# One layer of a hybrid diffusion block: another order in the prologue, and another RMSNorm in the tail

## The reference

```python
h = rmsnorm(x) * (1 + scale1) + shift1          # scale, shift, gate: SiLU(c) @ w_mod + b_mod
P = h @ W_in                                    # three token mixers and the merge gates
y_hy  = hyena_mix(...)                          # two long convolutions by FFT, see below
y_gla = gla(...); y_s5 = s5(...)
mix = W_out( sum_b sigmoid(g_b) * (y_b @ W_b) );  x += gate1 * mix
x += gate2 * SwiGLU(rmsnorm(x) * (1 + scale2) + shift2)
out = rmsnorm(x) * g_final

# a long convolution's filter k, for each of the two (cv = 0, 1):
h = (sin(...) @ w3) * exp(-t * |decay|)         # 512 positions x 512 channels, forward and backward
k = k * rsqrt(sum(k * k, axis=positions) + eps) # the filter's norm
k_f = rfft(k)                                   # the filter's spectrum
```

## Time and profile before

| | us |
|---|---|
| median of 3 runs | 1458.78 |
| lowest and highest | 1457.54, 1459.68 |
| profiled execution | 1453.09 |
| its span, first to last instruction | 1450.9 |
| mean granted clock of TensorE | 0.901 of full |

### The profile page before, as it was taken

The page is one execution under the profiler, slowest core; times in us unless marked ns, Lnnn a source line. Parts: engine busy times, 40 slices in busy tenths (PEclk is TensorE's granted clock), DMA queues, the critical chain, the costliest instruction groups (busy, mean ns, idle before and its releaser), DMA issues.

```text
span 1450.9 us, 15211 instructions
## 1 busy us (share of the span) xinstructions
PE 1219.5 (84%) x5929; PEld 919.3 (63%) x5929; DVE 562.8 (39%) x982; ACT 406.3 (28%) x722; POOL 403.3 (28%) x343
## 2 busy tenths in 40 slices
PE   4768998697657888888498989989679999999994
PEld 1335786685445667667364557649468888888883
DVE  3365324645456667566306381323230001100013
ACT  2454212332233333242041110111333222232221
POOL 2003132240211111021031111314135654556541
PEclk9986999798779888998599999989789999999997
DMA  9330132193201112130160214262513323333211
GB/s 331 112 133 0 59 117 75 32 200 121 72 28 50 34 36 80 25 95 20 41 202 15 102 44 145 87 210 80 152 51 88 115 80 93 103 89 115 81 51 58
DMA packets 137714, 131.48 MB, mean 91 GB/s; under 512 B 12985, under 2 KB 125817, under 8 KB 136620
## 3 DMA queue, kind: packets, MB, share of 16 engines
q1 hardware_dynamic: 125280, 103.48, 24.4%
q0 software_dynamic: 4416, 17.50, 3.5%
q10 hardware_dynamic: 7948, 9.54, 2.2%
HBM read 119.49 MB, written 8.91 MB: 89 GB/s over the span
## 4 chain that ended last, share of the span: by engine, by line
PE 56%; DVE 13%; ACT 5%; issue 3%; DMA 0%; ACTq 0%; DVEq 0%; POOL 0%; SPq 0%
PE psum L667 47%; PE psum L886 3%; PE psum L916 1%; PE psum L906 1%; PE psum L919 1%; PE psum L917 1%; PE psum L696 1%; DVE buf L1920 1%; DVE buf L1918 1%; PE psum L718 1%; DVE buf L1919 1%; ACT ring_hi L1339 1%; DVE hT_lo L2172 1%; DVE buf L1897 0%; DVE buf L1898 0%
## 5 line engine op out<-in xcount | busy, mean ns | idle before, releaser
L1185 POOL TENSOR_TENSOR ring_lo<-buf,ring_hi 128x512 fp32r<-128x512 f32 (+2 forms) x260 | 340.3, 1341 | 781.0 <-ACT ring_hi L1339 781.0
L667 PE MATMUL psum<-hT_hi,ring_hi 128*128 128x512 f32 x712 | 294.7, 414 | 25.8 <-POOL ring_lo L1185 15.2
L667 PE MATMUL psum<-hT_lo,ring_hi 128*128 128x512 f32 x712 | 284.1, 399 | 0.0
L667 PE MATMUL psum<-hT_hi,ring_lo 128*128 128x512 f32 x712 | 283.1, 398 | 0.0
L667 PE MATMUL psum<-buf,buf 128*128 128x512 f32 (+1 forms) x480 | 208.5, 589 | 30.3 <-DVE buf L2062 8.9
L1339 ACT ACTIVATE ring_hi<-buf 128x512 fp32r<-128x512 f32 (+2 forms) x260 | 139.7, 611 | 265.9 <-PE psum L667 197.4
L667 PEld LDWEIGHTS psum<-hT_hi,ring_hi 128*128 128x128 f32 x712 | 139.0, 195 | 60.3 <-POOL ring_lo L1185 15.6
L667 PEld LDWEIGHTS psum<-buf,buf 128*128 128x128 f32 x480 | 95.5, 201 | 128.0 <-issue 99.2
L667 PEld LDWEIGHTS psum<-hT_lo,ring_hi 128*128 128x128 f32 x712 | 138.4, 194 | 31.7 <-issue 3.6
L667 PEld LDWEIGHTS psum<-hT_hi,ring_lo 128*128 128x128 f32 x712 | 137.8, 194 | 29.8
L2181 DVE TENSOR_TENSOR buf<-psum,buf 128x512 f32<-128x512 f32 x22 | 15.2, 692 | 224.1 <-PE psum L667 224.1
(11 more groups left out here) (321 smaller groups left out, 1776.6 us busy)
## 6 DMA issues: line engine op xcount, KB each, us to landing
buf<-in_w_in SPq DMA_DIRECT2D x26, 1024.0 KB, 5.3
buf<-in_w_mod SPq DMA_DIRECT2D x24, 1024.0 KB, 6.0
buf<-in_w_ffn_in SPq DMA_DIRECT2D x44, 512.0 KB, 5.1
buf<-in_w_ffn_out SPq DMA_DIRECT2D x8, 1024.0 KB, 5.1
scr_k<-buf POOLq DMA_DIRECT2D x4, 1024.0 KB, 5.8
buf<-scr_k POOLq DMA_DIRECT2D x4, 1024.0 KB, 7.7
buf<-in_w_out SPq DMA_DIRECT2D x4, 1024.0 KB, 7.5
buf<-in_w_ffn_out SPq DMA_DIRECT2D x4, 768.0 KB, 4.4
```

Of the source, the lines that this page charges most:

```text
L667: ins = nc.tensor.matmul(o, a, b, start=start and n == 0, stop=stop and n == len(pairs) - 1)
L1185: nc.gpsimd.tensor_tensor(ring_lo[:, a:a + n], ring[:, a:a + n], ring_hi[:, h + i * n:h + i * n + n].bitcast(fp32), SUB)\
```

## The change

The step list is put in another order at two places, and three computations are written in another way.

**Prologue.** `x_sq` is cut into six calls that ACT issues between the exponentials of the first filter. `rms` stands after block 4 of the modulation, and its scaling of the tokens is a step `xn` of its own after `fnorm` of the first filter. All `modT` steps and `hT` now stand ahead of the first filter's `fspec`. The wait for the token splits moves from `hT` to `chan`. The second `filter` stands behind the k projection, its `fnorm` behind `vhalf(0)`, and its `fspec` behind `vhalf(1)`. `fnorm` now adds the eight squared tiles on DVE (two adds of 128x1024 into `Gp`, then one of 128x1024 and one of 128x512) and makes one product with the matrix of ones.

**Around the second norm.** Blocks 20 to 23 of the modulation and their `gt` steps are interleaved with the four `wo` steps, in the weight ring too, and `A2` follows `wo(0)`. The sum of squares is taken by ACT for each 256 columns as DVE finishes them. `norm2` runs for each token tile inside `wo(3)`. It no longer scales tokens: DVE writes the factor of each token on the diagonal of a 128x128 tile `diag`, and PE multiplies the residual by it, so that one float32 product both transposes and scales. The first four output blocks go token tile by token tile. The first `ffn` job waits for the splits one by one.

**Last products and final norm.** In the last chunk of each `down` the token tile is the outer loop. ACT squares halves of 512 columns after each `down_ev` of the second half, `final` runs for each tile inside the last `down_ev`, its last product is made in two halves, and SP stores each half (256 KB) instead of POOL.

```diff
-                      4: [("x_sq",), ("fnorm", 0)], 5: [("fspec", 0, 0)], 6: [("rms",), ("fspec", 0, 1)]}
+                      4: [("rms",)], 5: [("fnorm", 0), ("xn",)]}
...
-            if i == 4:
-                for k in range(4):
-                    step("modT", k)
...
-        for k in range(4, 8):
+        for k in range(8):
             step("modT", k)
         step("hT")
+        step("fspec", 0, 0)
+        step("fspec", 0, 1)
+        cols_slot("k", K0)
+        step("chan", "k", ("k0", "k1"), True)
         step("filter", 1, 0)
         step("filter", 1, 1)
-        cols_slot("k", K0)
-        step("chan", "k", ("k0", "k1"), True)
-        step("fnorm", 1)
         cols_slot("v0", V0)
         step("vhalf", 0)
+        step("fnorm", 1)
+        cols_slot("v1", V0 + 256)
+        step("vhalf", 1)
         step("fspec", 1, 0)
         step("fspec", 1, 1)
-        cols_slot("v1", V0 + 256)
-        step("vhalf", 1)
...
         for i in range(4):
             want(f"wo{i}", block(I["w_out"][0], 256 * i))
+            want(f"mod{20 + i}", block(w_mod, 256 * (20 + i)), split=False)
             step("wo", i)
-        step("norm2")
-        for i in (20, 21, 22, 23):
-            want(f"mod{i}", block(w_mod, 256 * i), split=False)
-            step("mod", i)
-            step("gt", i)
-        step("A2")
+            step("mod", 20 + i)
+            step("gt", 20 + i)
+            if i == 0:
+                step("A2")
         step("h2T")
...
             def fnorm(cv):
                 pe.wait_ge(S("ones"), 1)
-                pe.wait_ge(S("hsq"), 8 * cv + 8)
+                pe.wait_ge(S("hsum"), cv + 1)
...
-                close(product(o, ((ones, q[:, t, :]) for q in (Gp, Hp) for t in range(4))), name)
+                close(nc.tensor.matmul(o, ones, Gp[:, 0, :], start=True, stop=True), name)
...
             def h2_T():
-                pe.wait_ge(S("xn2"), 4)
-                for k in range(KD):
+                first = [open_job(f"x2T{k}") for k in range(4)]
+                for t in range(4):
+                    pe.wait_ge(S("diag"), t + 1)
+                    for k in range(4):
+                        ins = nc.tensor.matmul(first[k][:, t * P:(t + 1) * P], xr[:, t, k * P:(k + 1) * P],
+                                               diag[:, t, :], start=True, stop=True)
...
+            def x_sq(t):
+                if t == 0:
+                    act.wait_ge(S("x_in"), 32)
+                link(A(sqd, rowsx[t], ACT.Square, accum_out=ssq[:, t:t + 1]))
...
             def fnorm(cv):
+                for t in (0, 2):
+                    dve.wait_ge(S("hsq"), 8 * cv + 2 * t + 4)
+                    go(V.tensor_tensor(Gp[:, t:t + 2, :], Gp[:, t:t + 2, :], Hp[:, t:t + 2, :], ADD))
+                need(cnt[0])
+                link(V.tensor_tensor(Gp[:, 0:2, :], Gp[:, 0:2, :], Gp[:, 2:4, :], ADD))
+                V.tensor_tensor(Gp[:, 0, :], Gp[:, 0, :], Gp[:, 1, :], ADD).then_inc(S("hsum"), 1)
                 evacuated(dve, f"hn{cv}")
...
+            def norm2(t):
+                dve.wait_ge(S("ss2"), 12 + t + 1)
+                V.reduce_sum(ss2[:, t:t + 1], sq2[:, t, :], AX).then_inc(S("ms2"), 1)
+                dve.wait_ge(S("sd2"), t + 1)
+                link(V.reciprocal(rs2[:, t:t + 1], rs2[:, t:t + 1]))
+                V.tensor_scalar(diag[:, t, :], ident, rs2[:, t:t + 1], None, MUL).then_inc(S("diag"), 1)
...
+            def final(t):
+                dve.wait_ge(S("ssf"), 4 + t + 1)
+                V.reduce_sum(ssf[:, t:t + 1], sqf[:, t, :], AX).then_inc(S("msf"), 1)
+                dve.wait_ge(S("sdf"), t + 1)
+                link(V.reciprocal(rsf[:, t:t + 1], rsf[:, t:t + 1]))
+                for h in range(2):
+                    c = slice(512 * h, 512 * h + 512)
+                    V.scalar_tensor_tensor(xr[:, t, c], xr[:, t, c], rsf[:, t:t + 1], gfin[:, c], MUL, MUL)\
+                        .then_inc(S("out"), 1)
```

More of the change, by code:

```diff
@@ L1067, in ffn @@
                     o = open_job(name)
-                    close(product3(o, ((wh[:, k, :], wl[:, k, :], hT_hi[:, k, :], hT_lo[:, k, :])
-                                       for k in range(KD))), name)
+                    for k in range(KD):
+                        if name == "fa0":
+                            pe.wait_ge(S("h_split"), 2 * KD + k + 1)
+                        ins = product3(o, [(wh[:, k, :], wl[:, k, :], hT_hi[:, k, :], hT_lo[:, k, :])],
+                                       start=k == 0, stop=k == KD - 1)
+                    close(ins, name)
                 last_job[f"ffn{j}"] = f"fb{j}"
@@ L1080, in down @@
                 (wh, wl), = halves(slot)
-                for i in range(n):
-                    k = k0 + i
-                    pe.wait_ge(S("act_lo"), hf * NFH + k + 1)
-                    for t in range(4):
-                        c = slice(t * P, (t + 1) * P)
-                        ins = product3(acc[0][t], [(act_hi[:, k, c], act_lo[:, k, c], wh[:, i, :], wl[:, i, :])],
-                                       start=(k == 0), stop=(k == NFH - 1))
-                        if k == NFH - 1:
-                            close(ins, f"d{hf}{q}{t}")
+                last = k0 + n == NFH
+                if last:
+                    pe.wait_ge(S("act_lo"), (hf + 1) * NFH)
+                order = [(i, t) for t in range(4) for i in range(n)] if last else \
+                    [(i, t) for i in range(n) for t in range(4)]
+                for i, t in order:
+                    k = k0 + i
+                    if not last and t == 0:
+                        pe.wait_ge(S("act_lo"), hf * NFH + k + 1)
+                    c = slice(t * P, (t + 1) * P)
+                    ins = product3(acc[0][t], [(act_hi[:, k, c], act_lo[:, k, c], wh[:, i, :], wl[:, i, :])],
+                                   start=(k == 0), stop=(k == NFH - 1))
+                    if k == NFH - 1:
+                        close(ins, f"d{hf}{q}{t}")
                 if k0 + n < NFH:
@@ L1141, in _ @@
                     sp.dma_start(dst, src).then_inc(w_full[n % RS], 16)
+            for t in range(4):
+                for h in range(2):
+                    c = slice(512 * h, 512 * h + 512)
+                    sp.wait_ge(S("out"), 2 * t + h + 1)
+                    sp.dma_start(out[0, t * P:(t + 1) * P, c], xr[:, t, c]).then_inc(S("stored"), 16)
+            sp.wait_ge(S("stored"), 128)
         @block_.gpsimd
@@ L1515, in filt @@
                     A(fexp, adec[:, q, :], ACT.Exp, scale=tneg[:, t:t + 1]).then_inc(S("fexp"), 1)
+                    if cv == 0 and (q or t % 2):
+                        x_sq(2 + t if q else t // 2)
             def fnorm(cv):
```

129 lines of the change are left out of this document (69 added, 60 removed).

## The result

| | before | after |
|---|---|---|
| median, lowest and highest of 4 runs each, us | 1458.16 (1456.89 to 1459.68) | 1410.14 (1408.36 to 1415.64) |
| profiled execution, its span, us | 1453.09, 1450.9 | 1408.36, 1406.2 |
| mean granted clock | 0.901 | 0.907 |

A forecast was written before the change was run, and what follows sets the result against it. PE was taken to set the pace over most of the span, with gains at the edges where it waits or runs at 1.2 GHz. Gains 16.9 + 20.4 + 2.3 = 39.6 gave span 1411.3, median 1419, range 1407 to 1431.

The forecast's parts named there:

- Start to `z`: Prologue up to the start of `z` at 210.43: reordered steps and summing on DVE gain 16.9 us, bounds 9 to 22.
- The second filter: Prologue, 16 instructions: 6.8 us at full clock, 14.0 at half; taken as 9.4, plus 1.8 lost in products behind it.
- The first spectra: Prologue, on PE under ACT's scalings and DVE's splits: start at 81, cost 8.64 + 7.13 as before, k at 96.5.
- The bounds as named: Prologue gain: +4.6 and -2.6 for the filter's clock, +-3 for the first spectra, +2 for the store; 9 to 22.
- point of equality: The start of `z`, at 210.43 before: claimed the first point behind which both orders are equal.
- Last W_out product to the feed-forward: Second norm: 6.6 between W_out steps, 5.0 to first transpose, 21.4 after; 33.0 against 53.4, gain 20.4, bounds 15 to 24.
- The rule on transpose mode: Second norm: the skill's four-times-faster FP32 transposes would make the transposing products 14 us instead of 7.7, against the change.
- The end: Last chunk and final norm: DVE chain 11.6 after PE instead of 12.9, store 1.0 off; gain 2.3, bounds 0 to 5.
- The clock: Rival, prologue: second filter at half clock, v0 and v1 started so, first spectra late; 8 to 9 us more, 1428; 0.14.
- the dear product: Rival, second norm: transposing product costs four transposes, or POOL holds DVE through the splits; 6 us more, 1425; 0.08.
- The ring: Rival, W_out: PE stands still twice if weight load and split exceed 14 us; slower than before, 1460 or more; 0.02.
- Better than that: Rival: full clock in filter, transposes and first spectra, and a shorter end; about 10 us less, 1409; chance 0.13.

## Why the prediction was right, and where it was off

The points at which the work waits came as told in all three parts. The sizes were off in both directions, and the total is closer than its terms.

**Start to `z`, 16.9 forecast, 23.4 measured.** The order of events was as told: norm at 70.8, scalings at 73.85 (74.0), the wait of 7.92 (8.2) with the squares in it, and DVE's copies of a held by the store. Two terms were mis-sized. The second filter was 9.4 and 1.8 for a fall of the clock; it was 7.1 and nothing (-4.1). The failing step was the term's reason, that the filter, "with few rows like it", falls to half as `z` does: `z` has 32 rows, the filter 64, and the run with 32 rows gave the fall. The first spectra began at 79.75 instead of 81 and took 13.90 instead of 15.77 (-3.1); the stretches behind gave 0.7 back. The forecast's own sum has a slip here: 81 + 8.64 + 7.13 is 96.8, not 96.5. The spectra ran at full clock in one piece, where the earlier trace rows has them in two calls, the first of them behind a wait of 8.89 and with a granted clock of 0.59 over its first 4 us. The bounds as named (4.6, 3 and 2) would take 16.9 down to 7.3, not 9; the lower one was not needed, and the upper one of 22 was passed by 1.4. What made most of the gain is PE's shorter busy time, as the windows above show; the summing on DVE, put back in one run, is worth 6.0 of it at `z`.

**`z` itself, forecast at nothing.** The forecast set its point of equality at the start of `z`, but `z` was not equal behind it: it now falls to half clock from 189 on, as the granted clock shows, and takes 8.79 instead of 6.68 (-2.1). In the other profiles it takes 6.7 and 7.9 with the old prologue, 8.4 to 10.0 with the new one. Before it PE waits 1.70 for DVE, where it waited 0.82.

**Last W_out product to the feed-forward, 20.4 forecast with the W_out steps, 18.0 measured.** Three blocks at 2.2 came to 5.1 instead of 6.6, with some 1.7 of that this profile's clock; in the ten others with this code the stretch takes 68.7 to 69.3, 6.8 to 7.4 more than before, as forecast. To the first transposing product 4.6 (5.0). The transposing products 8.8 (9.5). The failing term is what stands behind them: 25.8 from their start to the end of the block, against 21.4. POOL's split was named, with its 1.63, and then taken to end in DVE's last pieces at no cost to PE. Four of DVE's pieces were slowed, PE waited 4.0 in all, and its clock fell to 0.58. Without POOL beside them the 25.8 are 20.3.

**The rule on transpose mode.** The timeline has 64 instructions of the change in 8.8 us, 3.74 / 32 = 0.117 each at full clock, so the estimate from the earlier trace rows (0.12) holds and no dear product is seen. By the Trainium skill, "TensorE: Matmul & The Clock Gate", section "Terms", which has transpose mode four times faster for FP32, the estimate had been 14 us; the measurement decides against it here. On the table load: 1390.62 + 1.28 = 1391.90, and the root begins at 1391.91, so no drain is seen behind the load; the Trainium skill, "ScalarE: Activation LUTs", section "What ACT_TABLE_LOAD costs", has one of 1.38.

**The end, 2.3 forecast, 6.1 measured.** DVE's chain was right, 11.2 after PE (11.6), bound by its waits for ACT as told (3.9 a tile, forecast 4.1). The store was mis-sized: 1.0, between 0 and 2.5, where it brought 4.5. The forecast named the half size and the new issuer together and had no row for either; the run with POOL's stores shows that 3.9 is the issuer.

**The rivals.** The clock did not eat the prologue, and the dear product did not come, though the other half of that rival, POOL holding DVE through the splits, did in part. The ring never held PE up between the W_out steps. It did once ahead of them: PE waited for POOL's half of the first W_out block. In the ten other kernels with the norm part this wait is 0 to 0.7, and that block begins 14.3 to 15.3 behind the first modulation block, in the changed kernel 14.3.

```profile
957.85 0.39 PE L670 MATMUL psum<-ring_hi,mT_hi 128*128 128x256 f32 x1 [1.93 <-POOL ring_lo L1210]
```

"Better than that" at 1409 named full clock in filter, transposes and first spectra, and a shorter end. It is nearest to what happened, at 1410.1, except that the transposing products began at 0.50. The errors of +6.5 and +3.8 were partly paid back by -2.4 around the second norm and -2.8 between `z` and W_out. That they cancel is luck, and the -2.8 is within the scatter of single profiles.

## What to carry to other kernels

A shared step list orders every engine at once: to take a wait away, find the one stream in which the work stands too late and move it there alone. Look who works beside DVE in a stretch that PE waits for, and hold GpSimd's work back if it can come later. A last store is worth issuing from SyncE, and a clock forecast for a product has to be taken from a row with the same number of rows and the same level at its entry.

## What the runs showed of the hardware

- Products of 64 rows kept the full clock for 20 us, and in the earlier trace rows stayed at 0.50 for 14 us; products of 32 rows fell from 1.00 to 0.50 in the same place.
- From DVE's last product to the end of the span pass 2.5 us with stores of 256 KB from SyncE (ten kernels), 6.4 with stores of 256 KB from GpSimd (one), 7.0 to 7.4 with stores of 512 KB from GpSimd (three).
- A casting subtraction of DVE over 128x512 takes 0.69 alone and 1.63 beside GpSimd's split.
- A float32 product of 128x128x128 takes two instructions of 0.117 us at full clock, one more than the transpose in the earlier trace rows.
- Where one profile had a wait of 1.5 us of PE that another had not, the clock fell twice behind it, and the stretch took 6.2 us longer; that the wait is the cause is not tested. Over the 750 us behind `z`, profiles of the same code differ by up to 9 us, and a gain of 3 to 5 us must be read at its own place, not in the span.
